# Opening of a fused two-block kernel: weights of both first columns by turns for each piece of x, and the fifth weight group split ahead of the gate functions

## The reference

```
def _swiglu(x, w_in, w_out):
    g, u = jnp.split(x @ w_in, 2, axis=-1)
    return (jax.nn.silu(g) * u) @ w_out

h = _swiglu(_rms_norm(x, ffn1_pre_norm[l]), ffn1_w_in[l], ffn1_w_out[l])
```

## Time and profile before

| | us |
|---|---|
| median of 3 runs | 890.25 (889.8 to 890.43) |
| the profiled execution, its own time | 890.23 |
| its span, first to last instruction | 888.5 |
| TensorE busy with matmuls | 879.5 (99%) |
| VectorE busy | 624.8 (70%) |
| ScalarE busy | 489.7 (55%) |

### The profile page before, as it was taken

The page is one execution under the profiler, slowest core; times in us unless marked ns, Lnnn a source line. Parts: engine busy times, 40 slices in busy tenths (PEclk is TensorE's granted clock), DMA queues, the critical chain, the costliest instruction groups (busy, mean ns, idle before and its releaser), DMA issues.

```text
span 888.5 us, 11475 instructions
## 1 busy us (share of the span) xinstructions
PE 879.5 (99%) x4628; PEld 752.0 (85%) x4628; DVE 624.8 (70%) x808; ACT 489.7 (55%) x661; POOL 64.5 (7%) x89
## 2 busy tenths in 40 slices
PE   8999999999999999999999999999999999999997
PEld 6888888888888888888888888888999888888886
DVE  6887776467767756577577777446979857888872
ACT  6855564445445556436565555435886544555551
POOL 2000000003021110000000000000390000000000
PEclk9999999999999999999999999999999999999999
DMA  9955555455753445455655555556534456555521
GB/s 349 357 190 190 190 191 199 154 190 175 285 197 120 187 163 178 184 190 190 237 190 189 190 190 190 189 187 245 184 109 177 149 185 258 190 190 191 190 94 48
DMA packets 26949, 169.89 MB, mean 191 GB/s; under 512 B 3617, under 2 KB 3665, under 8 KB 7953
## 3 DMA queue, kind: packets, MB, share of 16 engines
q1 hardware_dynamic: 24368, 161.23, 49.9%
q0 software_dynamic: 2240, 7.66, 2.5%
q10 hardware_dynamic: 288, 0.27, 0.1%
HBM read 167.05 MB, written 1.05 MB: 189 GB/s over the span
## 4 chain that ended last, share of the span: by engine, by line
PE 94%; DVE 3%; ACT 1%; DMA 1%; issue 1%; SPq 0%; DVEq 0%; ACTq 0%
PE acc L1640 15%; PE acc L1839 15%; PE acc L1642 15%; PE acc L1641 15%; PE acc L2102 8%; PE acc L1841 7%; PE acc L2104 4%; PE acc L1883 2%; PE acc L1655 2%; PE aux L2037 1%; PE aux L1764 1%; PE acc L1885 1%; PE aux L1642 1%; PE aux L1641 1%; PE aux L1640 1%; PE acc L2053 1%
## 5 line engine op out<-in xcount | busy, mean ns | idle before, releaser
L996 DVE TENSOR_TENSOR w_lo<-raw,w_hi 128x2048 fp32r<-128x2048 f32 x147 | 336.6, 2298 | 94.9 <-ACT w_hi L522 94.5
L522 ACT ACTIVATE w_hi<-raw 128x2048 fp32r<-128x2048 f32 x145 | 275.6, 1911 | 64.2 <-DMA raw<-weights 63.9
L1839 PE MATMUL acc<-xT,w_hi 128*128 128x512 f32 x576 | 200.4, 394 | 0.0
L1841 PE MATMUL acc<-xT,w_lo 128*128 128x256 f32 x576 | 159.7, 277 | 0.0
L1839 PEld LDWEIGHTS acc<-xT,w_hi 128*128 128x128 f32 x576 | 108.0, 188 | 25.0
L1640 PE MATMUL acc<-w_hi,xT 128*128 128x512 f32 x312 | 123.9, 397 | 0.0
L1642 PE MATMUL acc<-w_hi,xT 128*128 128x512 f32 x312 | 121.8, 390 | 0.0
L1641 PE MATMUL acc<-w_lo,xT 128*128 128x512 f32 x312 | 121.5, 390 | 0.0
L2102 PE MATMUL acc<-xT,w_hi 128*128 128x512 f32 x320 | 111.3, 394 | 0.0
L1841 PEld LDWEIGHTS acc<-xT,w_lo 128*128 128x128 f32 x576 | 108.2, 188 | 0.0
L2104 PE MATMUL acc<-xT,w_lo 128*128 128x256 f32 x320 | 88.7, 277 | 0.0
(11 more groups left out here) (263 smaller groups left out, 1289.6 us busy)
## 6 DMA issues: line engine op xcount, KB each, us to landing
raw<-weights SPq DMA_DIRECT2D x147, 1024.0 KB, 4.7
gain_pre<-gains POOLq DMA_DIRECT2D x5, 512.0 KB, 4.9
raw<-weights SPq DMA_DIRECT2D x4, 512.0 KB, 8.0
gain_post<-gains POOLq DMA_DIRECT2D x3, 512.0 KB, 5.5
gate_w<-gate_w_in POOLq DMA_DIRECT2D x1, 1536.0 KB, 9.0
x_turned<-x_turned_in SPq DMA_DIRECT2D x4, 256.0 KB, 5.6
x<-x_in SPq DMA_DIRECT2D x2, 512.0 KB, 11.7
bias_raw<-bias_in POOLq DMA_DIRECT2D x16, 64.0 KB, 3.1
```

The source lines that it names most:

```text
L522: a.activation(w_hi[:, g % RING], raw[:, g % RING], ACT.Copy).then_inc(hi_done, 1)
L996: v.tensor_tensor(w_lo[:, slot], raw[:, slot], w_hi[:, slot].bitcast(F32), ALU.subtract)\
L1839: m.matmul(dst, w_hi[:, slot, w], xT[:, k].rearrange("p a q -> p (a q)"), start=k == 0, stop=False)
L1841: i = m.matmul(dst[:, 0:S], w_lo[:, slot, w], xT[:, k, 0], start=False, stop=k == KD - 1)
```

## The change

Groups 1 and 2 trade places in the stream, so that group 1 is the first half of column 1 and group 2 the second half of column 0. In the opening, the first half of group 1 (`load_half(1, 0)`) is issued ahead of piece 1 of x and ahead of the second half of group 0; its second half ahead of pieces 2 and 3 of x. ScalarE, VectorE and TensorE take the halves in the same order, so that each piece of x meets the units of both columns. TensorE's waits for x go by the piece (`piece`), column 0 is complete after group 2, and `group_used` is raised after the second half of group 0 and in group 3 after its first unit. In `swiglu`, for the first feed-forward alone, `round_to(5)` and `low_to(5)` move ahead of `silu(0, 0, 0)` and `up(0, 0, 0)`.

```
+            def load_half(g, half):
+                part = slice(half * GROUP // 2, (half + 1) * GROUP // 2)
+                sp.dma_start(raw[:, g, part], weights[g - 1][:, part]).then_inc(landed[g] if half else part_landed[g - 1], 16)
+
             load_turned(0)
             for j in range(2):
                 sp.dma_start(raw[:, 0, j * UNIT:(j + 1) * UNIT], first_in[j]).then_inc(unit_landed[j], 16)
+            load_half(1, 0)
             load_turned(1)
             sp.dma_start(raw[:, 0, 2 * UNIT:].rearrange("p (j n) -> p j n", j=2),
                          first_in[2:4].rearrange("j p n -> p j n")).then_inc(landed[0], 16)
+            load_half(1, 1)
             for j in range(2, KD // 2):
                 load_turned(j)
-            for g in range(1, 3):
-                for half, done in enumerate((part_landed[g - 1], landed[g])):
-                    part = slice(half * GROUP // 2, (half + 1) * GROUP // 2)
-                    sp.dma_start(raw[:, g, part], weights[g - 1][:, part]).then_inc(done, 16)
+            load_half(2, 0)
+            load_half(2, 1)
...
                 act.wait_ge(gain0_landed, 16)
+                round_half(1, 0)
                 x_hi(1)
                 round_half(0, 1)
+                round_half(1, 1)
                 x_hi(2)
                 x_hi(3)
-                round_half(1, 0)
-                round_half(1, 1)
                 round_half(2, 0)
                 round_half(2, 1)
...
                 if g0 == 0:
+                    round_to(g0 + 5)
                     silu(0, 0, 0)
-                    round_to(g0 + 5)
                     silu(0, 0, 1)
                     silu(1, 1, 0)
...
                 low_unit(0)
                 low_unit(1)
+                low_half(1, 0)
                 x_lo(1)
                 low_half(0, 1)
+                low_half(1, 1)
                 x_lo(2)
                 x_lo(3)
-                low_half(1, 0)
-                low_half(1, 1)
                 low_half(2, 0)
                 low_half(2, 1)
...
                 if g0 == 0:
+                    low_to(g0 + 5)
                     up(0, 0, 0)
-                    low_to(g0 + 5)
                     up(0, 0, 1)
                     up(1, 1, 0)
...
                 def products(xT, w, g, t, units):
-                    column, half = divmod(g, 2)
+                    half, column = divmod(g, 2)
...
-                for g, units in ((0, (2, 3)), (1, (0, 1)), (1, (2, 3)), (2, (0, 1)), (2, (2, 3))):
-                    n = 2 * g + units[0] // 2
+                for g, units in ((1, (0, 1)), (0, (2, 3)), (1, (2, 3)), (2, (0, 1)), (2, (2, 3))):
+                    piece = 2 * (g // 2) + units[0] // 2
                     if units[0]:
                         pe.wait_ge(hi_done, g + 1)
                     else:
                         pe.wait_ge(half_hi, g)
-                    if g < 2:
-                        pe.wait_ge(turned_hi, 2 * n)
+                    if piece:
+                        pe.wait_ge(turned_hi, 2 * piece)
                     for t in range(T):
                         products(xT_hi, w_hi, g, t, units)
-                    if g < 2:
-                        pe.wait_ge(xn_ready, n + 1)
+                    if piece:
+                        pe.wait_ge(xn_ready, piece + 1)
...
-                        if n == 3:
+                        if g == 2 and units[0]:
                             i.then_inc(acc_full[t], 1)
-                    if n in (1, 5):
+                    if units[0] and g == 0:
                         i.then_inc(group_used, 1)
                 pe.wait_ge(lo_done, 4)
                 for t in range(T):
                     for unit in range(4):
                         i = product(acc[:, t, 1], xT_hi, xT_lo, 4 + unit, t, 3, unit, False, unit == 3)
+                        if t == 0 and unit == 0:
+                            i.then_inc(group_used, 1)
...
+    first = columns(a["ffn1_w_in"][0], ff)
     return np.concatenate([
-        columns(a["ffn1_w_in"][0], ff), pairs(a["ffn1_w_in"][0], ff_chunks), ...
+        first[[0, 2, 1, 3]], pairs(a["ffn1_w_in"][0], ff_chunks), ...
```

More of the change, by code:

```diff
@@ L1004, in low_half @@
             def low_half(g, half):
-                assert split[0] == g
+                assert split[0] == g or half == 0
                 slot, part = g % RING, slice(half * GROUP // 2, (half + 1) * GROUP // 2)
@@ L2151, in _stream @@
     a = {k: np.asarray(v) for k, v in inputs.items()}
+    first = columns(a["ffn1_w_in"][0], ff)
     return np.concatenate([
-        columns(a["ffn1_w_in"][0], ff), pairs(a["ffn1_w_in"][0], ff_chunks), rows(a["ffn1_w_out"][0]), columns(a["w_mix_in"][0], mix[:2]),
+        first[[0, 2, 1, 3]], pairs(a["ffn1_w_in"][0], ff_chunks), rows(a["ffn1_w_out"][0]), columns(a["w_mix_in"][0], mix[:2]),
         pairs(a["w_mix_in"][0], nqk), columns(a["w_mix_in"][0], mix[2:]),
```

## The result

The changed kernel takes 891.88 us (median of 17 runs, 891.14 to 893.99), the kernel before 890.25 (17 runs, 889.70 to 892.02): a ratio of 1.0020, 95% interval [1.0014, 1.0027]. Forecast were 889.6 and a range of 888.9 to 890.6. The change is slower by 1.6 us where a gain of 0.6 was expected. Measured twice more later, it stood at 1.0002 [0.9989, 1.0015] and 1.0017 [1.0008, 1.0025] to the kernel before.

The account below looks back on a forecast made before the run. TensorE was taken as the bound (94% of the chain), with 1.36 us to win at its opening wait. The sum: 890.23 - 0.61 at the opening, 0 behind it, = 889.62, median 889.6; range 888.9 to 890.6.

Parts of the forecast that it names:

- The opening: TensorE's loop at line 1655 starts at 9.09 instead of 9.70 us, a gain of 0.61 us.
- the midpoint of 7.98: ScalarE starts rounding group 1's first half at 7.98 us, halfway between 7.37 and 8.59 by the order of bytes.
- SyncE's waits: Groups 6 and 7 are released later but enter a queue that is still full: cost nothing.
- the table load: ScalarE's load ahead of the first gate function now follows group 4's rounding; nothing charged beyond 1.28 us.
- the columns: Column 0 is complete only after TensorE's fifth stage, at 22.6 us; the gate functions' products still come in time.
- The drain of 1.38 us: Rival, chance 0.04: a drain between group 4's rounding and the table load delays chunk 2 by 0.85 us; 890.5 us.
- in a row I take 0.38 from start to start, so they end at 26.45, 26.83 and 27.21: ScalarE's three gate functions after the table load run in a row, the last ending at 27.21 us.
- The 0.13 us on VectorE: VectorE starts group 5's low part at 29.03 instead of 28.90 us, 0.13 late.
- the 0.53 in hand at chunk 2: Chunk 0's up sum ends at 40.16 us, TensorE wants the bank for chunk 2 at 40.69: the tightest place.
- Given back at chunk 2: Rival, chance 0.11 (with nothing gained): VectorE is over 0.53 us later, TensorE waits at chunk 2; 889.6 to 890.2.
- 0 behind it: After the opening's -0.61 us, nothing more is gained or lost in the rest of the kernel.
- No named case reaches 1.8 us: No named case differs by 0.2% or 1.8 us; chances faster 0.03, within 0.94, slower 0.03.

Follow-up runs that it names:

- the variants with the new opening and the buffer: Changed kernel plus a second buffer for column 1's gate functions: 889.48, 890.27 us; with contiguous source for the half 889.62; with the half in two transfers 889.31, 888.99.

## Why the prediction was wrong

- **The opening: the bound was right, the number was met by luck.** TensorE's only wait in reach was the one at 9.70, and 0.61 us was forecast where the two profiles have 0.62. But this sets one execution of each kernel beside the other. In nine profiles of the new opening with the half in one piece, ScalarE's rounding of the half that TensorE waits for starts between 7.90 and 9.11 (median 8.32), in nine of the old one between 7.80 and 8.59 (8.24), each time straight after a wait for the transfer. TensorE's loop starts between 9.01 and 11.04 (9.43), against 8.91 to 9.70 (9.35). The kernel before was profiled at the late end of its starts (8.59 and 9.70), the changed one near the early end (7.95 and 9.06). So the midpoint of 7.98, taken from the order of the bytes, does not hold on average: 256 KB less ahead of the half did not make it land earlier in these profiles. The 0.5 us between the lower groups of times stands against this, and no run shows where they come from.
- **SyncE's waits, the table load, the columns: right.** No late group; the rounding ends at 24.78 and the load starts at 24.80. The drain of 1.38 us in the Trainium skill's ScalarE: Activation LUTs, What ACT_TABLE_LOAD costs, does not show here either.
- **The step that failed** is "in a row I take 0.38 from start to start, so they end at 26.45, 26.83 and 27.21". Two did (26.09 + 0.84 = 26.93, 0.1 later than forecast). The third ended at 28.00 instead of 27.21, since it waits for the product that reads the buffer it writes. I had listed what the gate functions wait for by the accumulators alone, and left out the wait for the reader of their own output, which stands in `silu` and in the old order had long been met. The 0.13 us on VectorE became 0.95, and the 0.53 in hand at chunk 2 a wait.
- **The rival was named, its price was not.** Given back at chunk 2, 0.11, if the products "come later than I reckon by over 0.53": it was that, at the place and by the engine named. I priced it at the wait alone, 889.6 to 890.2. The wait left only 0.18 of the 0.62; the slow pace behind it then cost 1.7 us more, and that no term of the sum held. In the profile the second feed-forward cost 1.66 in the same way. All of the loss beyond 890.2 is this: "0 behind it" in the sum left the pace out.
- **"No named case reaches 1.8 us"** failed for the same reason: the sum took TensorE's pace as given, and the kernel before already spread over 889.7 to 892.0 in 17 runs where three had shown 0.6.

Open stays what decides the pace. Shown is that, in every profile here, it changes only at breaks and then holds to the end of the first stage; that a wait of 0.3 to 0.9 us leads mostly to the slow one (35 of 41, 9 of 12, 11 of 12, 12 of 12 and 12 of 12 times above, against 55 of 180 in the kernel before; some of these have a slow later stage as well or instead), but not always; and that 8 of 56 times lie above in the variants with the new opening and the buffer, whose profiles have no wait in the first stage. A wait is not needed: a pause of 0.06 us was enough once, and in the profile with eight transposes chunk 1 was slow without any. Why the first 17 runs of the change had none below 891.1 and a later set had 5 of 12 is not explained. The openings of the profiles differ by over 1 us from run to run, and with them whether and how long chunk 2 waits.

## What to carry to other kernels

When work is moved ahead of another engine's step, list for each instruction behind it whom it waits for as the writer of a buffer, too: a wait that has always been met shows in no profile, and becomes the next one. Ask of a gain at the start of a stream where the next engine has its least slack; here 0.5 us in hand was used up, and 0.4 us of waiting and 1.7 us of slower pace for one stage stood against at most 0.6 won. Before an effect of half a microsecond at the start of a kernel is forecast from the landing of one transfer, profile the kernel more than once: here that time alone moved by 0.8 us from one execution of the kernel before and its variants to the next. And where single times lie in groups, count them by group before reading a median: three runs of one group tell nothing of the other.

## What the runs showed of the hardware

A stream of weight loads and matmuls that alternates 512 and 256 columns has two steady paces at the same granted clock of 1.00: 347 loads or 341 in 60 us (347 or 353 ns for a pair, from 88.74 and 90.44 us for 16 chunks of 16 pairs), with the same instructions and no wait in either. In the profiles the pace of the first stage changes only where the stream breaks, by a wait or by other matmuls, and holds from there to the end of the 18 chunks. One slow feed-forward is 1.7 us, and this goes with the two groups of times: all nine profiled executions above 890.8 us have a slow feed-forward (the changed kernel's first profile has two), and none of the eleven below has one. No execution of the kernel before in its upper group was profiled, so that its groups have this cause is inferred. And the same transfers at the start of a kernel land up to 1.2 us earlier or later from one execution to the next, as ScalarE's first rounding of a half shows, which each time starts straight after a wait for the transfer (7.90 to 9.11 us in the new opening with the half in one piece). Once, in the changed kernel with four more transposes, TensorE stood idle for 1.34 us in the opening. Its granted clock from 8 to 10 us was then 0.50, and four matmuls that took 1.20 us in the profile of the change took 1.98:

```profile
7.55 1.98 PE L1659 MATMUL acc<-w_hi,xT 128*128 128x512 f32 x4 [1.34 <-ACT w_hi L607]
```
